# Gated stages and the last down stage with 512-column products, the two halves of a gated sum added by one VectorE reduction from the bank

## What is computed

```
h = h + concat([ya, yb]) @ w_out[i]              # "mixed" stage of the kernel
e = rmsnorm(p[i] @ w_pe[i], pe_g[i])
h = h + e * sigmoid(h @ w_pg[i])                 # "gated" stage of the kernel
```

```
x = x + (silu(conv(h @ w_gate)) * (h @ w_up)) @ w_down    # D_FF = 5632; "down" stages
return rms_norm(x, final_norm_g)
```

## Time and profile before

| what | value |
|---|---|
| time, median of 3 runs | 2348.41 us (2348.26 to 2351.12) |
| the profiled execution's own time | 2350.31 us |
| its span in the profile | 2348.5 us |
| TensorE busy | 2262.1 us, 96% |
| VectorE busy | 1705.2 us, 73% |
| ScalarE busy | 1056.0 us, 45% |
| GpSimd busy | 560.4 us, 24% |
| mean granted TensorE clock | 0.979 of full speed |

### The profile page before, as it was taken

The page is one execution under the profiler, slowest core; times in us unless marked ns, Lnnn a source line. Parts: engine busy times, 40 slices in busy tenths (PEclk is TensorE's granted clock), DMA queues, the critical chain, the costliest instruction groups (busy, mean ns, idle before and its releaser), DMA issues. The chain is left out here.

```text
span 2348.5 us, 41000 instructions
## 1 busy us (share of the span) xinstructions
PE 2262.1 (96%) x15582; PEld 2035.3 (87%) x15582; DVE 1705.2 (73%) x2929; ACT 1056.0 (45%) x1392; POOL 560.4 (24%) x224
## 2 busy tenths in 40 slices
PE   6999989999999989999999898899999999999997
PEld 5888988998888978999999787688888888888897
DVE  4688658885888478888878655578888886556876
ACT  5445454444445554555545520344434443334443
POOL 3776631017776520110002301110000000000014
PEclk9999999999999999999999997799999999999999
DMA  6445434555545444444445300255555555555554
GB/s 213 180 163 175 151 134 172 183 187 189 186 161 175 144 146 178 180 176 171 157 160 182 90 2 2 72 191 185 185 190 183 192 181 195 181 194 180 195 201 176
DMA packets 69034, 384.93 MB, mean 164 GB/s; under 512 B 15088, under 2 KB 22768, under 8 KB 23984
## 3 DMA queue, kind: packets, MB, share of 16 engines
q1 hardware_dynamic: 68912, 383.22, 46.4%
HBM read 380.02 MB, written 3.18 MB: 163 GB/s over the span
## 5 line engine op out<-in xcount | busy, mean ns | idle before, releaser
L258 PE MATMUL ps<-opA,whi 128*128 128x512 f32 x2100 | 745.2, 395 | 0.9 <-issue 0.9
L228 ACT ACTIVATE whi<-raw 128x2048 fp32r<-128x2048 f32 x348 | 664.0, 1908 | 104.7 <-DMA raw<-weights_dram 102.9
L233 DVE TENSOR_TENSOR low<-raw,whi 128x2048 fp32r<-128x2048 f32 x254 | 582.4, 2293 | 76.2 <-ACT whi L228 48.6
L259 PE MATMUL ps<-opA,low 128*128 128x256 f32 x2240 | 603.8, 280 | 0.0
L240 POOL TENSOR_TENSOR low<-raw,whi 128x2048 fp32r<-128x2048 f32 x94 | 431.8, 4605 | 551.5 <-ACT whi L228 454.7
L258 PEld LDWEIGHTS ps<-opA,whi 128*128 128x128 f32 x2100 | 394.3, 188 | 91.6 <-issue 3.5
L259 PEld LDWEIGHTS ps<-opA,low 128*128 128x128 f32 x2240 | 420.7, 188 | 11.7
L258 PE MATMUL ps<-opB,whi 128*128 128x512 f32 x1020 | 367.9, 400 | 5.7 <-PEq L1970 4.3
L259 PE MATMUL ps<-opB,low 128*128 128x256 f32 x1088 | 295.3, 282 | 0.0
L267 ACT ACTIVATE crossed<-ps 128x256 f32<-128x256 f32 x152 | 58.4, 384 | 508.0 <-PE ps L261 508.0
L246 PE MATMUL ps<-opB,whi 128*128 128x256 f32 x944 | 271.4, 288 | 3.3 <-DVE ps L1381 2.2
(11 more groups left out here) (394 smaller groups left out, 3583.3 us busy)
## 6 DMA issues: line engine op xcount, KB each, us to landing
raw<-weights_dram SPq DMA_DIRECT2D x350, 1024.0 KB, 4.8
bias_t<-table_dram SPq DMA_DIRECT2D x16, 384.0 KB, 5.9
hT<-xT_dram SPq DMA_DIRECT2D x4, 512.0 KB, 9.9
out_dram<-hT SPq DMA_DIRECT2D x4, 512.0 KB, 2.9
lora_g<-lora_dram SPq DMA_DIRECT2D x1, 1024.0 KB, 5.3
p_in<-pT_dram SPq DMA_DIRECT2D x2, 256.0 KB, 2.9
lora_wa<-lora_dram SPq DMA_DIRECT2D x1, 512.0 KB, 6.1
chunk_mats_dram<-compact SPq DMA_DIRECT2D x4, 128.0 KB, 3.3
```

What stands on the lines that cost most here:

```text
L228: act.activation(whi[:, v % RING, :], raw[:, v % RING, :], ACT.Copy).then_inc(hi_done.sem, 1)
L233: v_.tensor_tensor(wlo(v % RING, 0, width), raw[:, v % RING, 0:width], whi[:, v % RING, 0:width].bitcast(F32), ALU.subtract).then_inc(lo_d ...
L258: pe.matmul(*cross, start=start, stop=False)
L259: mm = pe.matmul(ps[:, b, 0:T], wlo(s, w0, w0 + P), op[:, k, 0:T], start=False, stop=False)
```

## The change

Both gated stages and the last down stage are made with `wide=True`.

In a gated stage the halves are not added by way of `crossed`. VectorE, at the head of its body and ahead of the split of unit u+2, waits for the products of unit u and adds the halves with one `tensor_reduce`: it reads the 512 columns of the bank as 256 pairs, column t beside column t + 256, and writes 256 sums to bank 4 or 5. ScalarE's tanh waits for that sum and reads it there. In the first unit VectorE also waits for an earlier `ev_done`.

In the last down stage the path of the other wide stages is taken: ScalarE copies the right half (L267), VectorE adds it (L1048), and then does `residual_step`. In ScalarE's body that copy stands ahead of the square of the block before.

Two semaphores that nothing used are gone.

```diff
-        dve_chain, act_chain, pool_chain = Chain(sig("dve_step")), Chain(sig("act_step")), Chain(sig("pool_step"))
+        dve_chain, pool_chain = Chain(sig("dve_step")), Chain(sig("pool_step"))
...
-        stat_in, stat_mm, stat_ms, stat_rt, rs_done = (sig(n) for n in ("stat_in", "stat_mm", "stat_ms", "stat_rt", "rs_done"))
+        stat_mm, stat_ms, stat_rt, rs_done = (sig(n) for n in ("stat_mm", "stat_ms", "stat_rt", "rs_done"))
+        halves_added = sig("halves_added")
...
+        def add_halves(v, b, to):
+
+            return v.tensor_reduce(to, ps[:, b, :].rearrange("p (h t) -> p t h", h=2), axis=AX.X, op=ALU.add)
...
-            read = cross_read.ahead(KB) if wide else None
+            read = cross_read.ahead(KB) if wide and not gated else None
+            added = halves_added.ahead(KB) if wide and gated else None
...
                     if not isinstance(i, int) or u0 + m + LEAD < NU:
                         act_split(act, u0, j, i)
-                    if wide and (j + 1) % per_block == 0:
+                    if wide and not gated and (j + 1) % per_block == 0:
                         act_cross(act, u0, j, i, ((u0 + j) // per_block + flip) % 2, read)
...
                     if gated:
                         if isinstance(i, int) and m == 0:
                             act.wait_ge(ev_done.sem, u0 + 2)
-                        act.wait_ge(mm_done.sem, 4 * i + (u0 + j + 1))
-                        act.activation(t1[:, 0:T], ps[:, (u0 + j) % 2, 0:T], ACT.Tanh, scale=0.5).then_inc(ev_done.sem, 1)
+                        act.wait_ge(added.sem, added.base + 4 * i + j + 1)
+                        act.activation(t1[:, 0:T], ps[:, 4 + (u0 + j) % 2, 0:T], ACT.Tanh, scale=0.5).then_inc(ev_done.sem, 1)
...
                     if not isinstance(i, int) or u0 + m + LEAD < NU:
+                        if gated:
+                            v.wait_ge(mm_done.sem, 4 * i + (u + 1))
+                            if isinstance(i, int) and m == 0:
+                                v.wait_ge(ev_done.sem, u0 + 2)
+                            add_halves(v, u % 2, ps[:, 4 + u % 2, 0:T]).then_inc(added.sem, 1)
                         dve_split(v, u0, j, i)
...
             gated = phase_residual(u, opnd[cur], opnd[1 - cur], in2_gain if last else par_of("norm_g", l + 1), gated=True,
-                                   squares=1 + last, ready=mixed.written)
+                                   squares=1 + last, ready=mixed.written, wide=True)
...
-        down2 = phase_residual(u, act_hl, None, par_of("final_g2"), kb=FF_CHUNKS[1], squares=1, ready=up2.written)
+        down2 = phase_residual(u, act_hl, None, par_of("final_g2"), kb=FF_CHUNKS[1], squares=1, ready=up2.written, wide=True)
```

## The result

| what | before | changed |
|---|---|---|
| time, median (10 runs each, same chip) | 2349.95 us | 2364.48 us |
| lowest to highest | 2337.79 to 2362.54 | 2356.14 to 2427.65 |
| profiled execution | 2350.31 us | 2365.67 us |
| its span | 2348.5 us | 2363.9 us |
| mean granted clock | 0.979 | 0.975 |

The ratio is 1.0052, with a 95% interval of 1.0033 to 1.0072: the changed kernel is slower by 0.52%, or 12.2 us (7.8 to 16.9).

What follows compares the result with a forecast made beforehand. VectorE's body, lengthened by the reduction, was taken to bound both gated stages. Terms +0.8, +9.9 and -0.2 gave +10.5 us on the profiled 2350.31, so 2360.8; that execution lay 1.9 above the median, so 2358.9 us, range 2352.5 to 2367.

Steps and rivals of the forecast that it cites:

- What bounds the stages: Gated stages: TensorE sets the first's pace, VectorE already the second's, 5.85 us against 5.76; with the reduction VectorE bounds both.
- The reduction's price: VectorE in both gated stages: one reduction costs 0.60 us from start to start, between 0.33 and 1.13.
- First gated stage: VectorE's body becomes 5.73 us against TensorE's 5.61; the last operand block comes late, +0.8 us.
- The turn of the loop: VectorE in the gated stages: each loop turn adds 0.30 us, three times a stage.
- Second gated stage: VectorE's body goes from 5.85 to 6.45 us; the running sum and statistic come later with no cover, +9.9 us.
- near 1051: Sign after the second gated stage: the time at which TensorE's statistic would stand, 1040.25 before.
- Last down stage: Wide products save 1.8 us, the last block's tail costs 1.65 us; -0.2 us in all, between -1.8 and +1.5.
- The -1.8 of the products: Last down stage: 16 units of 12 k save 0.115 us each, -1.8 us, if VectorE keeps up.
- Rival 1: Gated stages: the reduction is cheap, 0.33 us; sum +3.2, 2351.6 us, no change by the measure; chance 8%.
- Rival 2: Gated stages: reading halves 256 columns apart, or restarting for each result, is slow, 1.13 us; +16, 2375 us; chance 8%.
- Rival 3: First gated stage: GpSimd's addition meets no VectorE operation, body 5.36 us, TensorE sets the pace; +7.3, 2355.7 us; chance 14%.
- Rival 4: All three stages: the change keeps its promise, TensorE sets every pace; -5 us, 2343.5 us; chance 2%.

Runs made afterwards that it cites:

- e8_store_narrow: Kernel before, with only the copy of the new h moved from VectorE to ScalarE in the gated stages; -5.0 us in the changed stretches.
- e1_first_gated: Kernel before, with wide products and the reduction in the first gated stage alone; that stretch +0.6 us, by time not told from no change.
- e6_copy_path: Changed kernel, but in the gated stages ScalarE copies the right half and VectorE adds it, without the reduction; 2356.59 us, ratio 1.0027 to the kernel before.
- e5_split_first: Changed kernel, with the split of unit u+2 put ahead of the wait and the reduction; 2381.58 us, ratio 1.0131 to the kernel before.
- e7_store_on_act: Changed kernel, with the copy of the new h moved from VectorE to ScalarE, behind the squares; faster by 0.3% than the kernel before.
- e2_second_gated: Kernel before, with wide products and the reduction in the second gated stage alone; that stretch +9.3 us, by time told from no change.
- e9_both: Changed kernel, with the halves added by way of ScalarE's copy and the copy of the new h on ScalarE; 2349.05 us, ratio 0.9975 to the kernel before.
- e4_double: Changed kernel, with the reduction made twice in both gated stages; 2377.82 us, ratio 1.0117 to the kernel before.

## Why the prediction was right, point by point

**What bounds the stages** held. In the second the body went from 5.85 to 6.37, and TensorE waits for L234, as said. The doubled reduction shows the same for the first stage.

**The reduction's price.** 0.60 from start to start was forecast, 0.61 measured, 700 ns in all against 690. That is the price by the 512 elements read; nothing is left over for the 256 results or for the distance of 256 columns within a pair. No run varied the pattern, so that is a reading of one number. The rule of the Trainium skill ("VectorE: DVE Perf Modes", "The DRAIN you can't avoid") would have added 0.09 to each, and that would make 2.6 us. The rows don't show it: the reduction of 451.57 ends at 452.27, the split starts at 452.18. The same section adds that an instruction which nothing holds starts earlier, and that is what they show.

**First gated stage**: forecast +0.8, measured +0.6 alone and +1.4 in the whole. The term hid two errors that cancel in part. The body was put at 5.73 and took 5.65, because the reduction starts 0.32 after the store of h starts, not the 0.40 that a split waited there. The turn of the loop was put at 0.30 and took 0.47, and the body behind it another 0.09: I took it from one turn of the second stage before, 6.15 against 5.85. 14 bodies and 3 turns gave 81.1, the trace has 532.27 - 451.57 = 80.7. The final matmul was forecast for 536.85, which is 538.15 in this trace (the stage began 1.3 later), and stands at 538.10. The wait of 2.6 us for the last block is in the forecast's working. Missed was what it can set off: in the changed kernel the clock fell behind it, for 0.8 us, and in `e1_first_gated` it did not.

**Second gated stage**: forecast +9.9, measured +9.3. The first two reductions were put at 946.2 and 952.7, that is 950.8 and 957.3 here; they stand at 950.70 and 957.36. The body again is 0.08 under the forecast (6.37, not 6.45), 14 of them 1.1 us; the turns, with the longer bodies behind them, give 0.5 back. What follows makes nothing good, as said, but not on the path that was named. The prediction let the delay run by GpSimd's running sum to TensorE's statistic. In the changed kernel TensorE didn't wait for that sum, and in both kernels the statistic lay ready long before VectorE used it: the delay runs down VectorE's own queue. Both paths begin at VectorE's last block, so the sum came out the same; `e8_store_narrow` is where the difference shows (-5.0 for -2). The sign "near 1051" for the statistic was also off by the prediction's own sum, which gives 1050.2; it stands at 1049.5.

**Last down stage**: forecast -0.2, measured -0.2, alone and in the whole. Pace 4.20 and tail 1.52, where 4.205 and 1.65 were forecast. The -1.8 of the products is there, and 1.5 of it is given back behind the last unit.

**The rivals.** Rival 1 (cheap reduction) was false for this instruction; `e6_copy_path`, with one that is cheap, comes near its sum, +2.5 against +3.2, by terms that miss in opposite ways. Rival 2 fell with the 0.70. Rival 3 fell in the first stage, where the addition still meets L953 in fifteen of sixteen units; but `e5_split_first` and `e6_copy_path` show that it hung on the order of the instructions, and that the contention goes elsewhere rather than away. I had taken "it meets nothing" as its only other outcome. Rival 4, TensorE's pace everywhere, is what `e7_store_on_act` reaches once L960 is gone: the 5.85 that barred it held a removable copy.

**The time.** 2358.9 stands against 2364.48 of the runs and 2365.67 of the profile. The 10.5 was right for the three stages, in part because errors in them offset each other. Of the 5.6 us by which the median lies above the forecast, 1.5 is the kernel before itself, whose median rose from 2348.41 (3 runs) to 2349.95 (10 runs). The profiled pair's other 4.9 us I did not forecast, and the kernel before differs from itself by more, in the same stretches and with its granted clock. `e2_second_gated`, which has the larger part of the change, shows 2070.4 elsewhere, before's own value. So nothing shows that any of it follows from the change; that a small part does is not ruled out.

## What to carry to other kernels

Before a product is made wider, add up the body of the engine that clears the bank, instruction by instruction from start to start: at 86% busy it was the bound already, though TensorE stood at 98%, and each 0.1 us put into it cost 0.1 us a unit. When an engine waits for another in the middle of its body, put its one long independent instruction between the request and the use, as the split here covers the tanh; moving it left 0.57 us idle in each body and, with the contention that moved along, cost 9 to 12 us a stage. And a copy that nobody waits for belongs on an engine with time to spare: here 1.1 us of contention sat on one such copy, and by the stretches moving it was worth 5.0 us where all the wider products add 1.9. A saving in such a place has to be measured: where GpSimd runs beside, a shorter step can bring the next one under its addition, as in `e9_both`.

## What the runs showed of the hardware that was not expected

- A `tensor_reduce` from PSUM over pairs 256 columns apart, 512 elements to 256 sums, takes 0.70 us, and the next instruction starts 0.61 behind it.
- VectorE beside GpSimd's addition: the h store took 1.38 for 0.28, L953 0.86 for 0.48, the split 3.31 for 2.28; or GpSimd paid, 3.18 for 1.30, when the split had begun first (`e8_store_narrow`, 990.10). The reduction was not stretched (0.70 at 991.20, the addition from 990.53 to 991.83). The Trainium skill ("SBUF — State Buffer", "Who interferes with whom") says that on trn2 `tensor_reduce` never contends with GpSimd, that a subtraction with both inputs in SBUF does, and that whoever issues first blocks the other; these rows agree.
- After the same wait of 2.6 us TensorE went on at its higher level of 2.4 GHz in one trace (`e1_first_gated`, L262 in 0.40 us, granted clock 1.00 from 537 to 541) and at half, 1.2 GHz, in another (the changed kernel, 0.63, then 1.05 for two statistic matmuls that take 0.59, granted clock 0.57). After 3.2 us it was at half too (`e4_double`, L262 in 0.63).
- The same code in one stretch had granted clocks of 0.81 to 0.97 from trace to trace: 15 us, more than the whole change.
